# Differential attention in a one-core backbone: keys and queries rotated in place during the projections, heads written out one by one

## The reference

```
q, k, v = split(x @ w_in, 3)              # 8 heads, 2 maps of width 64 each, values of width 128
ql, kl = apply_rope(ql), apply_rope(kl)   # latent tokens only, pairs (x1, x2) turned by row and column angle
keys, vals = concat([kc, kl]), concat([vc, vl])
s = einsum(q, keys) * 64**-0.5; p = softmax(s)
a = p[map 0] - lam * p[map 1]             # lam from four learned vectors
o = einsum(a, vals)
y = (rmsnorm(o, subln) * (1 - lam_init)).reshape(T, D) @ w_out
```

## Time and profile before

| | |
|---|---|
| device time, 3 runs | median 2550.07 us (2547.52 to 2555.49) |
| the profiled execution | 2550.66 us, span 2549.0 us |
| PE busy | 2421.8 us (95%) |
| DVE busy | 828.5 us (33%) |
| ACT busy | 528.4 us (21%) |
| POOL busy | 195.4 us (8%) |
| mean granted TensorE clock | 0.978 |

### The profile page before, as it was taken

How to read it: one execution, slowest core, us unless ns; L and a number is a source line. 1 busy time by engine, 2 the same in 40 slices (tenths; PEclk the granted TensorE clock), 3 DMA queues, 4 the chain that set the end, 5 groups by cost and what they waited for, 6 DMA issues and landing times.

```text
span 2549.0 us, 31145 instructions
## 1 busy us (share of the span) xinstructions
PE 2421.8 (95%) x12399; PEld 1977.2 (78%) x12399; DVE 828.5 (33%) x1600; ACT 528.4 (21%) x1305; POOL 195.4 (8%) x268
## 2 busy tenths in 40 slices
PE   5999999999998999899999999999999999678998
PEld 3788888864556988778888888888888867367887
DVE  4233310164545777253333013433301200731001
ACT  2111110122233444331111103111110211431001
POOL 1100000001022232000001000000000000100000
PEclk7999999999999999999999999999999999988999
DMA  8554462412210000134446523522452231023462
GB/s 271 199 174 156 163 169 73 136 53 81 67 50 17 1 1 1 50 117 148 165 151 192 168 68 106 186 95 82 128 136 68 89 116 66 0 66 119 158 173 62
DMA packets 277449, 275.56 MB, mean 108 GB/s; under 512 B 6505, under 2 KB 258019, under 8 KB 277219
## 3 DMA queue, kind: packets, MB, share of 16 engines
q1 hardware_dynamic: 256611, 198.60, 25.6%
q0 software_dynamic: 20736, 75.51, 8.4%
HBM read 273.04 MB, written 1.05 MB: 108 GB/s over the span
## 4 chain that ended last, share of the span: by engine, by line
PE 91%; DVE 4%; ACT 3%; issue 2%; DMA 1%; SPq 0%; POOL 0%; POOLq 0%; DVEq 0%; ACTq 0%
PE bank L714 32%; PE bank L859 18%; PE bank L609 12%; PE bank L879 6%; PE bank L905 3%; PE bank L1026 2%; PE bank L681 2%; PE bank L587 2%; PE bank L1185 2%; PE bank L1033 2%; PE bank L964 1%; PE bank L1040 1%; PE bank L989 1%; ACT hs L1571 1%; DVE room L2003 1%
## 5 line engine op out<-in xcount | busy, mean ns | idle before, releaser
L859 PE MATMUL bank<-big,ring 128*128 128x256 f32 x2112 | 458.8, 379 | 0.0
L859 PEld LDWEIGHTS bank<-big,ring 128*128 128x128 f32 x2112 | 400.4, 190 | 53.9
L714 PE MATMUL bank<-hs,ring 128*128 128x256 f32 x1584 | 378.3, 384 | 1.3 <-ACT hs L1316 1.3
L714 PEld LDWEIGHTS bank<-hs,ring 128*128 128x128 f32 x1584 | 300.1, 192 | 52.2 <-issue 11.3
L714 PE MATMUL bank<-room,big 128*128 128x256 f32 x1056 | 252.5, 382 | 0.0
L609 PE MATMUL bank<-hs,ring 128*128 128x512 f32 (+2 forms) x592 | 231.6, 548 | 0.0
L714 PEld LDWEIGHTS bank<-room,big 128*128 128x128 f32 x1056 | 201.8, 192 | 28.1 <-DVE room L1780 0.5
L2188 DVE TENSOR_TENSOR room<-room 128x256 f32<-128x256 f32 x70 | 29.8, 425 | 521.0 <-ACT room L1607 521.0
L609 PEld LDWEIGHTS bank<-hs,ring 128*128 128x128 f32 (+1 forms) x592 | 109.8, 188 | 107.6 <-issue 104.1
L472 POOL DMA_DIRECT2D mring<-in_w_mod x144 | 76.2, 529 | 1084.1 <-PE bank L587 1009.8
L879 PE MATMUL bank<-hs,ring 128*128 128x256 f32 x704 | 153.9, 382 | 1.6 <-ACT hs L1316 1.6
(11 more groups left out here) (277 smaller groups left out, 2826.2 us busy)
## 6 DMA issues: line engine op xcount, KB each, us to landing
ring<-in_ffn_w_in SPq DMA_DIRECT2D x88, 1024.0 KB, 5.0
mring<-in_w_mod POOLq DMA_DIRECT2D x144, 512.0 KB, 5.4
ring<-in_ffn_w_out SPq DMA_DIRECT2D x44, 1408.0 KB, 7.0
ring<-in_gdn_w_in SPq DMA_DIRECT2D x16, 1024.0 KB, 5.5
ring<-in_diff_w_in SPq DMA_DIRECT2D x12, 1024.0 KB, 5.1
ring<-in_gdn_w_out SPq DMA_DIRECT2D x4, 1024.0 KB, 4.9
ring<-in_diff_w_out SPq DMA_DIRECT2D x4, 1024.0 KB, 4.9
cst<-in_consts SPq DMA_DIRECT2D x1, 1344.0 KB, 9.5
```

What stands on the lines that cost most here:

```text
L714: last = mm(bank[:, (g0 + b) % 4, 0:LAT], w[:, k, jj * P:(jj + 1) * P], rhs[:, k, :], start=start and k == 0, stop=(k == KC // 2 - 1), ski ...
L859: last = mm(bank[:, g % 4, 0:LAT], w[:, k, :], big[:, k, cols], start=(k == 0), stop=(k == FC - 1))
```

## The change

During the projections PE turns back each key and query chunk two groups after its own (`turn_back(i)`, i from 0 to 15, into bank 4 or 5 by turns), and DVE writes the rotated chunk over the unrotated one in `big` (`rotary(i)`). `qrot`, `kall` and `vhead` are gone with POOL's copies: the scores read queries and keys, and the product the values, where they lie. On all engines the eight heads are written out one by one. The output of a head and its sum go to bank 0 or 1 by turns; `oat` and `rat` are double. DVE's order is now maxima(h), mix(h); ACT takes the next head's first two exponentials, then this head's output, then the other two, then the root. The first scores are placed ahead of the wait for lambda.

```diff
@@ -297,28 +297,17 @@
...
         carve = Carver(room, ROOM)
-        qrot = carve(LAT)
-        rtmp = carve(2, LAT)
-        rtmp2 = carve(2, LAT)
-        vhead = [carve(NC, P), carve(NC, P)]
-        kall = [carve(TOK), carve(TOK)]
+        rtmp = [carve(LAT), carve(LAT)]
+        rtmp2 = [carve(LAT), carve(LAT)]
         amix = carve(2, TOK)
...
         stat = [carve(24), carve(24)]
-        oat = carve(LAT)
-        rat = carve(LAT)
+        oat = [carve(LAT), carve(LAT)]
+        rat = [carve(LAT), carve(LAT)]
         lam_prod = amix[:, 0, 0:2 * HALF].rearrange("p (a b) -> p a b", a=2)
...
         v_rows = flat_big[:, 2 * KC * TOK:3 * KC * TOK].rearrange("p (t d) -> p t d", t=NC)
-        def heads_of(loop, body):
-            with loop(HEADS // 2 - 1) as it:
-                for par in range(2):
-                    body(it * 2 + par, par, True)
-            body(HEADS - 2, 0, True)
-            body(HEADS - 1, 1, False)
         def chunks(a):
@@ -529,30 +518,10 @@
             mod_loads(1)
-            def k_fix(n, par):
-                nc.gpsimd.tensor_copy(kall[par][:, 0:CTX].unsqueeze(1), big[:, ds(n + KC, 1), 0:CTX]).then_inc(S["k_fixed"], 1)
-            def v_fix_rows(n, par):
-                nc.gpsimd.tensor_copy(vhead[par], v_rows[:, :, ds(n * P, P)]).then_inc(S["v_fixed"], 1)
-            def head_leaves(n):
-                of("attn_root", n, 1, 1)
-                nc.gpsimd.tensor_tensor(big[:, ds(n + 3 * KC, 1), 0:LAT], oat.unsqueeze(1), rat.unsqueeze(1), ALU.mult
-                                        ).then_inc(S["head_closed"], 1)
             pool.wait_ge(S["head_closed"], HEADS + 2)
-            for par in range(2):
-                k_fix(par, par)
-                v_fix_rows(par, par)
-            with pool.Fori(0, HEADS // 2 - 1) as it:
-                for par in range(2):
-                    of("scores_done", it * 2 + par, 4, 4)
-                    k_fix(it * 2 + (par + 2), par)
-                    of("attn_done", it * 2 + par, 1, 1)
-                    v_fix_rows(it * 2 + (par + 2), par)
-                    head_leaves(it * 2 + par)
-            head_leaves(HEADS - 2)
-            head_leaves(HEADS - 1)
+            for h in range(HEADS):
+                of("attn_root", h, 1, 1)
+                nc.gpsimd.tensor_tensor(big[:, h + 3 * KC, 0:LAT], oat[h % 2], rat[h % 2], ALU.mult).then_inc(S["head_closed"], 1)
         @block.tensor
@@ -1163,6 +1132,16 @@
                 if kind == "diff":
+                    def turn_back(i):
+                        pe.wait_ge(S["acc_freed"], g0 + i + 1 + 4)
+                        if i > 1:
+                            pe.wait_ge(S["rotated"], i - 1)
+                        x = big[:, KC + i, CTX:TOK] if i < KC else big[:, i - KC, 0:LAT]
+                        mm(bank[:, 4 + i % 2, 0:LAT], k_("rot"), x, start=True, stop=True).then_inc(S["turned_back"], 1)
+                    for i in range(2):
+                        turn_back(i)
                     for part in range(2):
@@ -1174,6 +1153,7 @@
...
                                       cols=LAT if part == 1 else TOK, starts=(jj == 0))
+                                turn_back(part * 8 + 2 * r + jj - 2)
                     for r in range(4):
@@ -1187,50 +1167,48 @@
...
                             last.then_inc(S["acc_done"], 1)
+                            if r == 0 and t < 2:
+                                turn_back(2 * KC - 2 + t)
                     def of(sem, n, per, k):
                         pe.wait_ge(S[sem], n * per + k)
-                    def turn_back(n):
-                        mm(bank[:, 0, 0:LAT].unsqueeze(1), k_("rot"), big[:, ds(n, 1), 0:LAT], start=True, stop=True)
-                        mm(bank[:, 0, LAT:2 * LAT].unsqueeze(1), k_("rot"), big[:, ds(n + KC, 1), CTX:TOK],
-                           start=True, stop=True).then_inc(S["turned_back"], 1)
-                    def scores(n, par, first=False):
-                        of("k_fixed", n, 1, 1)
-                        of("rotated", n, 2, 2)
+                    def scores(n):
                         for t in range(2):
...
                                 rows = slice(m * HALF, (m + 1) * HALF)
-                                if not first:
+                                if n:
                                     of("probs_done", n - 1, 4, 2 * t + m + 1)
-                                mm(bank[:, 4 + 2 * t + m, :], qrot[rows, t * P:(t + 1) * P], kall[par][rows, :], start=True, stop=True).then_inc(S["scores_done"], 1)
-                    def one_head(h, par, more):
-                        if more:
-                            turn_back(h + 1)
-                            scores(h + 1, 1 - par)
+                                mm(bank[:, 4 + 2 * t + m, :], big[rows, n, t * P:(t + 1) * P], big[rows, n + KC, :],
+                                   start=True, stop=True).then_inc(S["scores_done"], 1)
+                    def attend(h):
                         for t in range(2):
                             of("mixed_done", h, 2, t + 1)
+                            if h:
+                                of("a_copied", h - 1, 2, t + 1)
                             for kt in range(NC):
...
                         of("a_copied", h, 2, 2)
-                        pe.wait_ge(S["v_fixed"], h + 1)
+                        if h > 1:
+                            of("attn_root", h - 2, 1, 1)
                         for kt in range(NC):
-                            last = mm(bank[:, 1, 0:LAT], vhead[par][:, kt, :], at_[:, kt, :], start=(kt == 0), stop=(kt == NC - 1))
+                            last = mm(bank[:, h % 2, 0:LAT], v_rows[:, kt, h * P:(h + 1) * P], at_[:, kt, :],
+                                      start=(kt == 0), stop=(kt == NC - 1))
                         last.then_inc(S["attn_done"], 1)
                         of("attn_squared", h, 1, 1)
-                        mm(bank[:, 1, LAT:2 * LAT], ones, rat, start=True, stop=True).then_inc(S["attn_sum"], 1)
+                        mm(bank[:, h % 2, LAT:2 * LAT], ones, rat[h % 2], start=True, stop=True).then_inc(S["attn_sum"], 1)
+                    pe.wait_ge(S["rotated"], 2 * KC)
+                    scores(0)
                     pe.wait_ge(S["head_closed"], HEADS + 2)
-                    turn_back(0)
-                    scores(0, 0, first=True)
-                    heads_of(lambda n: pe.Fori(0, n), one_head)
+                    pe.wait_ge(S["acc_freed"], g0 + 32 + 4)
+                    for h in range(HEADS):
+                        if h + 1 < HEADS:
+                            scores(h + 1)
+                        attend(h)
                     pe.wait_ge(S["head_closed"], 2 * HEADS + 2)
@@ -1564,35 +1542,44 @@
                         act.wait_ge(S[sem], n * per + k)
-                    def exps(n, par):
-                        for k in range(4):
+                    def exps(n, ks):
+                        st = stat[n % 2]
+                        for k in ks:
                             of("max_done", n, 4, k + 1)
-                            fn(probs[par][:, k, :], bank[:, 4 + k, :], ACT.Exp, bias=stat[par][:, 4 + k:5 + k], scale=HALF ** -0.5,
-                               accum_out=stat[par][:, 8 + k:9 + k]).then_inc(S["probs_done"], 1)
-                    def one_head(h, par, more):
+                            fn(probs[n % 2][:, k, :], bank[:, 4 + k, :], ACT.Exp, bias=st[:, 4 + k:5 + k], scale=HALF ** -0.5,
+                               accum_out=st[:, 8 + k:9 + k]).then_inc(S["probs_done"], 1)
+                    def copy_a(h):
                         for t in range(2):
                             of("a_turned", h, 2, t + 1)
+                            if h:
+                                of("attn_done", h - 1, 1, 1)
                             fn(at_[:, :, t * P:(t + 1) * P], bank[:, 2 + t, :].rearrange("p (k q) -> p k q", k=NC),
                                ACT.Copy).then_inc(S["a_copied"], 1)
+                    def leave(h):
+                        of("attn_done", h, 1, 1)
+                        if h > 1:
+                            act.wait_ge(S["head_closed"], h + (HEADS + 1))
+                        fn(oat[h % 2], bank[:, h % 2, 0:LAT], ACT.Copy, scale=lamv[:, 6:7])
+                        fn(rat[h % 2], bank[:, h % 2, 0:LAT], ACT.Square).then_inc(S["attn_squared"], 1)
+                    def root(h):
+                        of("attn_sum", h, 1, 1)
+                        inv_root(rat[h % 2], bank[:, h % 2, LAT:2 * LAT], eps_col[:, 0:1], 1.0 / P).then_inc(S["attn_root"], 1)
+                    exps(0, range(4))
+                    act.wait_ge(S["head_closed"], HEADS + 2)
+                    for h in range(HEADS):
+                        more = h + 1 < HEADS
+                        copy_a(h)
                         if more:
-                            exps(h + 1, 1 - par)
-                        of("attn_done", h, 1, 1)
```

(75 more changed lines are left out.)

4 lines of the change are left out of this document (2 added, 2 removed).

## The result

| | before | changed |
|---|---|---|
| device time, 4 runs | median 2552.40 us (2547.52 to 2555.49) | median 2530.13 us (2528.38 to 2534.83) |
| span of the profiled execution | 2549.0 us | 2526.5 us |
| projections' last matmul to the output projection | 101.7 us | 71.3 us |

The changed kernel takes 0.9917 of the time of before, 95% interval 0.9898 to 0.9936: 0.8% faster. 2531 was forecast. The gain between the medians is 22.3 us, between the profiled spans 22.5.

A forecast was written before the change was run, and what follows sets the result against it. Projections bound by PE's work, attention by a chain passing between engines. 2164.8 + 8.8 + 7 x 7.4 + 6.9 = 2232.3, with 8.0 clock loss 2240.3, 19.3 us earlier: 2531 us, range 2518 to 2543.

The forecast's parts named there:

- Turn-backs: Projections: 16 added PE matmuls at 0.43 us each, 6.9 us; upper end 0.70 each if every wait empties the array.
- Start: Attention's start: lambda is late, then four maxima and two mixes; 8.8 us to the end of head 0's second mix.
- One head: Steady attention head: 7.2 us through ACT and DVE, 7.4 through PE's own order; 7.4 taken.
- POOL's part at nothing: Attention: POOL's key and value copies go at nothing; its multiplication is on the path only behind the last head.
- The clock: Attention: half-clock losses of 3 us at the start, 2.5 in the body and 2.5 at the tail, 8.0 together.
- Sum: Output projection's start: 2232.3 at full clock, 27.3 us earlier; with clock losses 2240.3, 19.3 us earlier.
- rival 1: Attention: the clock holds everywhere, output projection 27.3 us earlier and 2.1 more gained in it, 2521 us; chance 0.17.
- The time: Whole kernel: 2550.66-19.3-0.6 = 2530.8, so 2531 us.
- Signs: DVE 20 to 33 us busy in projections; sums over ones 7.4 us apart; attention near 75 us, PE's share above 0.75.
- Instruction supply: Attention: heads written out on four engines are each held up by 1 us, 8 in all, 2539 us; chance 0.08.
- rival 2: Attention's body: half clock in a third of it, 9.0 us a head, about 2540 us; chance 0.13.
- rival 4: Attention's body: PE's order stays at half clock, 12.1 us a head, slower at 2562 us; chance 0.03.

The follow-up runs named there:

- run 1: Changed kernel with POOL's multiplication at a head's end waiting until DVE has mixed both halves of the next head; 2525.97 us in its one run.
- run 4: Changed kernel with rotation put back into the heads, no turn-backs in the projections, and one output bank, oat and rat; 2543.08 us in one run.
- run 3: Changed kernel with one output bank, one oat and one rat, with the waits that belong to them; attention 75.7 us.
- run 2: Changed kernel with ACT taking all four exponentials of the next head before reading this head's output; 2523.85 us in one run.
- run 5: Changed kernel with PE issuing the scores of the head after next before this head's sum over ones; 2527.81 us in one run.
- run 6: Changed kernel with scores of the head after next before the sum over ones, and four undivided exponentials before the output's reading; median 2517.63 us.
- run 7: Changed kernel with early scores, undivided exponentials and the output projection's first 11 matmuls in the last head's PE gaps; median 2512.22 us, 0.9869 of before.

## Why the prediction was right

Counted from the projections' start, which came 1.3 us later in the changed kernel's execution for reasons that lie ahead of the change:

- *Turn-backs.* 0.43 us each, 6.9 in all; measured 117.4 against 110.5 us. None empties the array. Right.
- *Start.* 8.8 us to the end of head 0's second mix; measured 2174.61-2166.08 = 8.5. Right, and lambda was what was late.
- *One head.* 7.2 through ACT and DVE, 7.4 through PE; I took 7.4. Measured 7.21 without and 7.68 with a collision that no term had. The 7.21 is PE's order, as forecast (run 1); its sum was 0.2 too long, as eight transposes in a row take 1.09 us (2181.38), not 1.32. From the third head on the other circuit binds, which is 7.14 by itself. The missing term is POOL's multiplication beside DVE's last mixing operation, 0.54 us; run 1 took it away. Over seven heads the body is 53.3 us, against 51.8 without the clock's share.
- *POOL's part at nothing.* Wrong for the multiplication: it is on no chain by its waits, yet it held up DVE. For the copies no wait shows a cost, but in the kernel before they met DVE too, as these rows show. The cosine product (L2137) takes 0.83 beside POOL's copy (L536), 0.42 alone.

```profile
2189.76 0.42 DVE L2136 TENSOR_TENSOR room<-big,cst 128x256 f32<-128x256 f32 x1 [0.29 <-issue]
2189.79 0.87 POOL L536 COPY room<-big 128x512 f32 x1 [6.87 <-PE bank L1224]
2190.10 0.83 DVE L2137 TENSOR_TENSOR room<-big,cst 128x256 f32<-128x256 f32 x1
```

Likewise the rotation's sums (L2141, L2142), on which the scores wait, take 0.46 and 0.61 at 2193.36 and 2193.74 (such a sum takes 0.41 by itself in run 4), where POOL's multiplication and copy run (2192.82, 2193.48). The mixing operation was spared: 0.75 in all 16 cases. The prediction's way of looking, at waits alone, could not see this.
- *The clock.* I charged 3 at the start, 2.5 in the body, 2.5 at the end. The body never fell; the end did, as priced; the start is open from one execution to the next: full clock in both profiled executions of the changed kernel, half in runs 1 and 3. In run 3 it cost 1.1 + 3.7 = 4.8 us up to the second product, more than my upper end of 4.0. The body's charge was wrong in its reason and made up for the collision by chance.
- *Sum.* Counted from the projections' start, the output projection was to come 19.3 us earlier and came 23.5 earlier: 3.3 of the difference is the start, 1.0 the body. So the gain in this stretch lies midway between the forecast and rival 1's 27.3.
- *The time.* The forecast stood on 2550.07 for the kernel before, the median of three runs; with the fourth it is 2552.40. The gain was 22.3 us between the medians, 3 more than I had added up and 1.3 less than in the stretch above, as the projections started later. That 2531 came within 1 us of 2530.13 is in part luck.
- *Signs.* Two that I had named fell short: DVE 19.0 us busy in the projections (20 to 33), PE's share of the attention 0.71 (above 0.75). Sums over ones were 7.68 apart, not 7.4, the attention 71.3 us, not 75.

Of the rivals, the first (the clock holds everywhere) came true for the start and the body, not for the last head. Instruction supply is out: the engines' gaps between the written-out heads all end with another engine (only weight loads, which run beside the matmuls, have waits that nothing ends). Half clock in the body (rivals 2 and 4) did not occur in any profiled execution with the rotation outside the heads, between the start and the last head; in run 4, with PE less busy, it was there again (eight transposes from 2189.82 took 1.93 us, 1.09 at full clock). The section of the Trainium skill on depth-cycling of PSUM banks ("TensorE: Matmul & The Clock Gate") does not describe the steady heads here: PE has gaps of 0.3 to 0.8 us between its groups in each, and products and transposes keep their lengths of the full clock.

Of the change's parts, the rotation's move carries most: 14 to 19 us net of the turn-backs, against 4.9 for POOL's copies, the written-out heads, ACT's order and the early first scores together (run 4). Double buffers bring nothing (run 3). Divided exponentials bring nothing as things stand, 0.48 us a head where the collision is gone (runs 1 and 2), and a loss once the scores stand ahead of the sum over ones (runs 5 and 6).

## What to carry to other kernels

Where engines hand one unit of work round, add up every closed circuit, each engine's own order included; an edit that shortens one and lengthens another shows nothing until its counterpart is made. An operation that nobody waits for still costs when it meets another engine's that reads SBUF as well: look at durations, not only at waits. The gaps of a chain's last turn are a place for the next stage's first work.

## What was not expected of the hardware

DVE's operation with two SBUF inputs and POOL's multiplication delay each other: 0.75 us becomes 1.29 for DVE, or 0.72 becomes 1.25 for POOL, while DVE's reductions from PSUM (0.68) run beside POOL undisturbed. The Trainium skill has this, in "SBUF — State Buffer", section "Who interferes with whom": DVE with two SBUF inputs contends with a GpSimd instruction that reads SBUF, the shared port pair is an exclusive lock, the order of issue decides who blocks, and reductions never contend. The trace agrees on who contends; on the order it does so at 2181.00, where DVE starts 0.09 us ahead and POOL is prolonged. In the six later heads DVE's recorded start is 0.01 to 0.02 us ahead and DVE is prolonged, so starts that close do not tell the order.

The half clock at the attention's start, with the same instructions and gaps, came in two of the eight profiled executions that begin the attention alike (runs 1 and 3, not the changed kernel's two nor runs 2, 5, 6 and 7). In these two the last value group ended at 2161.4 and 2161.6 us of the span, in the other six between 2165.3 and 2166.4. What links the two, if anything, is open.
